# Two transformer blocks on one core: the second block's attention, gate and first query in another order

## The reference, cut to what matters

```python
x = rms(x, final_norm)                               # end of the first block
h = rms(x, ln_mix_g)
u, v, q, k, vb = split(h @ w_in_2)                   # 5 x 512 columns
# gate: per block of 128 tokens and group g of 64 columns
v  = rms(gelu(v), gmlp_norm_g)
sp = einsum('gij,bnjgc->bnigc', masked w_s, v) + b_s
a  = gelu(u) * sp
# band attention: 8 heads of 64, chunks of 64 see themselves and 8 before
q, k = rms per head (q, q_g), rms per head (k, k_g)
p  = softmax(q k^T / 8 + rel_bias, masked)
x  = x + concat(a, p @ vb) @ w_out_2
# experts: 8 heads choose 16 of 16384 experts for each token
qq = rms(x, ln_ffn_g) @ w_query                      # 2048 columns
sc = qq . sub_keys;  16 best of 128, twice;  16 best of the 256 sums -> eidx, g = softmax
x  = x + sum_k g_k * gelu(u[eidx_k] . rms(x)) * v[eidx_k]
```

## Time and profile before

| | |
|---|---|
| median of 3 runs | 1234.54 us |
| the profiled execution's own time | 1229.8 us |
| its span, first to last instruction | 1228.1 us |
| TensorE busy | 1066.6 us (87%) |
| VectorE busy | 809.1 us (66%) |
| ScalarE busy | 614.0 us (50%) |
| GpSimd busy | 344.3 us (28%) |
| mean granted TensorE clock | 0.975 of full speed |
| DMA moved | 369.54 MB, 301 GB/s |

### The profile page before, as it was taken

One profiled execution on the slowest core, in us unless ns is written; L12 is line 12 of the kernel. 1 busy time (PEld: TensorE's weight loads), 2 busy tenths in 40 slices (PEclk: granted clock), 3 DMA queues, 4 the chain that ended last, 5 costly groups with the idle time before them and its releaser, 6 DMA issues.

```text
span 1228.1 us, 12558 instructions
## 1 busy us (share of the span) xinstructions
PE 1066.6 (87%) x3760; PEld 664.6 (54%) x3760; DVE 809.1 (66%) x1669; ACT 614.0 (50%) x1340; POOL 344.3 (28%) x288
## 2 busy tenths in 40 slices
PE   6999999999999999999878988777778777778686
PEld 5788878788878777877434443323223323233232
DVE  4763666665545677567786677766776677677744
ACT  6464554454445456656555544544344434544453
POOL 1000000200000000016556444444545454555440
PEclk9999999999999999899999999999999998989999
DMA  8453447765625653336999999999999999999995
GB/s 309 138 198 111 138 144 237 262 201 176 188 87 193 220 203 101 140 137 232 422 421 422 421 421 421 422 421 419 422 422 415 422 415 408 409 413 423 422 420 244
DMA packets 95253, 369.54 MB, mean 301 GB/s; under 512 B 6544, under 2 KB 30104, under 8 KB 62304
## 3 DMA queue, kind: packets, MB, share of 16 engines
q0 software_dynamic: 38176, 273.46, 54.0%
q1 hardware_dynamic: 57024, 95.44, 23.3%
HBM read 367.81 MB, written 1.06 MB: 300 GB/s over the span
## 4 chain that ended last, share of the span: by engine, by line
PE 48%; DMA 24%; DVE 15%; ACT 6%; issue 3%; POOL 1%; DVEq 0%; SPq 0%; ACTq 0%
DMA uv_ring<-in_peer_uv,expert 24%; PE gemm L1633 12%; PE gemm L1312 10%; PE gemm L1314 10%; PE gemm L1313 10%; DVE uv_ring L1228 4%; PE trb L1306 1%; DVE w_lo L769 1%; ACT w_hi L440 1%; POOL uv_ring L418 1%; ACT diag L739 1%; PE mmb L1392 1%; DVE hit L1218 1%; PE mmb L1433 1%; DVE hit L1216 1%
## 5 line engine op out<-in xcount | busy, mean ns | idle before, releaser
L1633 PE MATMUL gemm<-uv_ring,diag 128*128 128x512 f32 x1024 | 499.0, 632 | 126.6 <-ACT diag L739 126.4
L1633 PEld LDWEIGHTS gemm<-uv_ring,diag 128*128 128x128 f32 x1024 | 192.1, 199 | 421.1 <-ACT diag L739 246.2
L1228 DVE CUSTOM_DVE_ANT_0 uv_ring<-uv_ring,xn 128x1024 f32<-128x1024 f32 x256 | 310.1, 1222 | 160.3 <-DMA uv_ring<-in_peer_uv,expert 159.8
L418 POOL DMA_INDIRECT uv_ring<-in_peer_uv,expert x256 | 317.5, 1240 | 324.2 <-PE gemm L1633 302.6
L769 DVE TENSOR_TENSOR w_lo<-raw,w_hi 128x1024 fp32r<-128x1024 f32 (+1 forms) x197 | 208.6, 1072 | 167.8 <-ACT w_hi L440 167.1
L440 ACT ACTIVATE w_hi<-raw 128x1024 fp32r<-128x1024 f32 (+1 forms) x204 | 189.1, 939 | 198.0 <-PE gemm L1314 195.7
L1312 PE MATMUL gemm<-w_hi,hT_hi 128*128 128x512 f32 (+1 forms) x608 | 247.0, 406 | 16.7 <-DVE w_lo L769 15.6
L1314 PE MATMUL gemm<-w_hi,hT_lo 128*128 128x512 f32 (+1 forms) x608 | 237.5, 391 | 0.0
L1313 PE MATMUL gemm<-w_lo,hT_hi 128*128 128x512 f32 (+1 forms) x608 | 236.9, 390 | 0.0
L733 ACT ACTIVATE hid_g<-hid,scales 128x1 f32<-128x1 f32 x256 | 75.1, 293 | 312.0 <-DVE hid L1228 309.9
L1312 PEld LDWEIGHTS gemm<-w_hi,hT_hi 128*128 128x128 f32 x608 | 115.5, 190 | 44.0 <-DVE w_lo L769 17.0
(11 more groups left out here) (203 smaller groups left out, 776.9 us busy)
## 6 DMA issues: line engine op xcount, KB each, us to landing
raw<-in_w_in SPq DMA_DIRECT2D x31, 1024.0 KB, 5.2
raw<-in_w_gate SPq DMA_DIRECT2D x22, 512.0 KB, 3.9
raw<-in_w_up SPq DMA_DIRECT2D x22, 512.0 KB, 4.9
raw<-in_w_down SPq DMA_DIRECT2D x22, 512.0 KB, 3.2
raw<-in_w_out SPq DMA_DIRECT2D x8, 1024.0 KB, 5.0
raw<-in_peer_w_query SPq DMA_DIRECT2D x8, 1024.0 KB, 5.0
raw<-in_w_ret_o SPq DMA_DIRECT2D x4, 1024.0 KB, 5.1
uv_ring<-in_peer_uv,expert POOLq DMA_INDIRECT x256, 14.4
```

Source lines behind the costliest of these rows:

```text
L418: nc.gpsimd.indirect_dma_start(out=uv_ring[k % RING][:], out_offset=None, in_=peer_uv, in_offset=bass.IndirectOffsetOnAxis(ap=expert[:, n, ...
L1228: V.tensor_tensor_reduce(out=u_row, in0=u_row, in1=xn[:, b, :], scale=1.0, scalar=0.0, op0=ALU.mult, op1=ALU.add, accum_out=hid[par][:, k: ...
L1633: last = nc.tensor.matmul(gemm[2 * b + n][:], diag[k % 4][:], uv_ring[k % RING][:, D + n * CHUNK:D + (n + 1) * CHUNK], start=(begin and k ...
```

## The change

It reorders, with these parts:

- norm2 and norm4: the remainders of quarters 2 and 3 of C_FF and C_QUERY are VectorE's and stand before the gain of tile 1; at norm2 tile 0's inverse root stands after tile 1's columns, and TensorE turns tile 1 before quarter 3 instead of quarter 2.
- norm3 and C_IN2 + 1: quarters of roundings and remainders stand between the columns, the squares and the roots.
- Band: the turns of q and k and the score jobs stand between the parts of C_IN2 + 3 and C_IN2 + 4. The turned k is ScalarE's, as before.
- The probabilities are turned undivided; the division is in the eviction of the attention result, now VectorE's. They are turned before the gate product.
- Gate: 8 matmuls of 128 columns (both tiles), evicted by 8 fused operations (add the bias, multiply by u) into `proj2`; `sq` isn't used and `mixed_a_ready` goes. TensorE order: gate, values of tile 0, turns, values of tile 1, C_OUT2.
- ScalarE makes tile 1's exponentials after the gelu of v and its squares.
- GpSimd loads the keys once the band's q and k are normed.
- C_QUERY: tile 0's four quarters first, then tile 1's turns, tile 0's query turned, its key scores, then tile 1.

```diff
-            remainders(C_FF, (2, 3))
-            pool.wait_ge(mixed_a_ready, TB)
+            pool.wait_ge(qk_normed, TB)
             pool.dma_start(keys_t[:], peer_keys_t).then_inc(keys_landed, 16)
-            remainders(C_QUERY, (2, 3))
             remainders(C_QUERY + 1, (1, 2, 3))
...
# ScalarE, norm_behind
+                hi_at(c + 1, quarters=(2, 3))
                 squares(0, 1)
-                hi_at(c + 1, quarters=(2, 3))
-                root_of(name, 0)
-                residual_in(c, 1)
-                hi_columns(name, (2, 3))
-                squares(1, 1)
-                root_of(name, 1)
+                if name == "norm4":
+                    root_of(name, 0)
+                else:
+                    residual_in(c, 1)
+                    hi_columns(name, (2, 3))
+                    root_of(name, 0)
+                    squares(1, 1)
+                    root_of(name, 1)
...
# ScalarE, second block
+            hi_at(C_IN2, quarters=(0, 1))
             hi_columns("norm3", (0, 1))
-            hi_at(C_IN2)
+            hi_at(C_IN2, quarters=(2, 3))
...
+            hi_at(C_IN2 + 3)
+            in2_out(2)
+            key_columns(0)
             hi_at(C_IN2 + 4, quarters=(0,))
+            key_columns(1)
+            hi_at(C_IN2 + 4, quarters=(1,))
             softmax_exp(2, 0)
-            hi_at(C_IN2 + 4, quarters=(1,))
-            softmax_exp(2, 1)
             hi_at(C_IN2 + 4, quarters=(2, 3))
+            in2_out(3, ACT.Gelu_apprx_tanh)
...
+            softmax_exp(2, 1)
             root("gate", TB)
             nc.scalar.preload_act_table(ACT.Gelu_apprx_tanh)
+            probs_columns((0, 1))
+            in2_out(4, ACT.Gelu_apprx_tanh)
+            probs_columns((2, 3, 4, 5))
             hi_at(C_OUT2)
...
             queries_out(0, 0)
+            residual_in(C_OUT2 + 1, 1)
+            hi_columns("norm4", (2, 3))
             query_columns(0, 0)
-            hi_at(C_QUERY + 1, quarters=(0,))
+            squares(1, 1)
+            root_of("norm4", 1)
             scores_out(0, 0)
-            hi_at(C_QUERY + 1, quarters=(1, 2, 3))
+            hi_at(C_QUERY + 1)
...
# VectorE, norm_behind
+                lo_at(c + 1, quarters=(2, 3))
+                if name == "norm4":
+                    variance(name, 0)
+                    inverse_root(0, 1, RS[name], dst=scales[:, at:at + 1], done=scale_ready)
                 gained(1, 0, row)
-                variance(name, 0)
-                inverse_root(0, 1, RS[name], dst=scales[:, at:at + 1], done=scale_ready)
                 residual(c, 1, (1,), scale)
                 gained(1, 1, row)
                 lo_columns(name, (2, 3))
+                if name == "norm2":
+                    variance(name, 0)
+                    inverse_root(0, 1, RS[name], dst=scales[:, at:at + 1], done=scale_ready)
...
# VectorE, second block
             down_in(0)
+            lo_at(C_IN2, quarters=(0,))
             lo_columns("norm3", (0, 1))
-            lo_at(C_IN2, quarters=(0, 1))
+            lo_at(C_IN2, quarters=(1,))
             down_in(1)
...
+            lo_at(C_IN2 + 3, quarters=(0,))
+            query_band(0)
+            lo_at(C_IN2 + 3, quarters=(1,))
+            query_band(1)
+            lo_at(C_IN2 + 3, quarters=(2, 3))
+            band_scores((0, 1))
+            band_max(0, 2)
+            lo_at(C_IN2 + 4, quarters=(0,))
+            band_scores((2, 3))
+            lo_at(C_IN2 + 4, quarters=(1,))
+            band_scores((4, 5))
+            band_max(1, 6)
+            lo_at(C_IN2 + 4, quarters=(2, 3))
...
-            finish_softmax()
...
+            def band_out(b):
+                m = MM["o_band"] + b
                 dve.wait_ge(mm_filled, m + 1)
+                V.tensor_tensor(proj2[:, b, D:D + HALF]..., mmb[m % 2][:]..., den[:, b, :].unsqueeze(2).to_broadcast([P, HEADS, HD]), ALU.mult)
+            for n in range(2):
+                m = MM["gate"] + n
+                for g in range(4):
+                    u = proj2[:, :, (4 * n + g) * HD:(4 * n + g + 1) * HD]
+                    V.scalar_tensor_tensor(out=u, in0=mmb[m % 2][:, g * P:(g + 1) * P]..., scalar=gains[:, G_BS + ...], in1=u, op0=ALU.add, op1=ALU.mult)
+            lo_at(C_OUT2, quarters=(0, 1))
+            band_out(0)
+            lo_columns("mixed", (0, 1))
+            lo_at(C_OUT2, quarters=(2, 3))
+            band_out(1)
+            lo_columns("mixed", (2, 3))
...
# TensorE
-            product_at(C_FF, by_tile=True, ready=columns_ready("norm2"), before={(2, 0): norm_columns("norm2", 1)})
+            product_at(C_FF, by_tile=True, ready=columns_ready("norm2"), before={(3, 0): norm_columns("norm2", 1)})
...
+            product_at(C_IN2 + 3, before={(0, 0): lambda: turn_band(0, 0), (0, 1): lambda: turn_band(0, 1), (1, 0): lambda: turn_band(1, 0),
+                                          (1, 1): lambda: turn_band(1, 1), (2, 0): lambda: score_band((0, 1)), (3, 0): lambda: score_band((2, 3))})
+            product_at(C_IN2 + 4, before={(0, 0): lambda: score_band((4, 5))})
+            for n in range(6): ... turn(TR["p_band"] + n, ...)
+            for n in range(2):
+                bank = mm_bank(MM["gate"] + n)
+                for g in range(4):
+                    at = HALF + (4 * n + g) * HD
+                    nc.tensor.matmul(bank[:, g * P:(g + 1) * P], ws_t[:, 4 * n + g, :], proj2[:, :, at:at + HD], start=True, stop=True)
+            band_values(0)
+            columns("mixed", mixed_rows, (0, 1))
+            band_values(1)
+            product_at(C_OUT2, before={(1, 0): lambda: columns("mixed", mixed_rows, (2, 3))}, ready=columns_ready("mixed"))
...
             product_at(C_QUERY, by_tile=True, ready=columns_ready("norm4"),
-                       before={(2, 0): norm_columns("norm4", 1), (1, 1): lambda: turn_queries(0, (0,)), (2, 1): lambda: key_scores(0, (0,))})
+                       before={(0, 1): lambda: (norm_columns("norm4", 1)(), turn_queries(0, (0,)), key_scores(0, (0,)))})
```

133 lines of the change are left out of this document (64 added, 69 removed).

## The result

The changed kernel takes 1212.24 us by the median of 4 executions (1211.61 to 1212.95), the kernel before 1233.91 on the same chip (1228.26 to 1236.47); the ratio is 0.9839, 95% interval [0.9815, 0.9864]. The forecast was 1222.5 with a range of 1217.5 to 1229: the direction was right, the gain about twice what I had said. The changed kernel's profiled execution took 1212.02 us (span 1210.2, granted clock 0.98) against 1229.8, so the traces explain 17.8 of the 21.7 us between the medians.

The account below looks back on a forecast made before the run. TensorE was taken to bound the work ahead of the first gather, DMA the 660 us after it. Five gains sum to 14.1 us, less 2 set aside; 12 off the median 1234.54 gives 1222.5, range 1217.5 to 1229.

Parts of the forecast that it names:

- The median of the runs shown is 4.7 above that execution; less 12: Whole kernel: 12 us taken off the median 1234.54, which lay 4.7 above the profiled execution, gives 1222.5.
- Against it I set 2: Allowance against the summed gains: 1.7 us for a clock fall on the gate's chain, 0.3 for releases rounded off.
- Rival A: Whole kernel: everything in the sum and no clock fall, 14 to 15 us off, 1220; chance 0.15.
- The sum of the parts: Ahead of the first gather: five gains of 3.9, 2.0, 2.6, 5.2 and 0.4 us, 14.1 together.
- Part 4: Last band product to C_OUT2's first matmul: division at eviction, earlier turns and a shorter gate save 5.2 us.
- Part 2: Second block's input (norm3): an earlier start and no wait at the next product save 2.0 us.
- part 5: norm4 and first query product: tile 0's query first saves 0.4 us, select then held by a remainder.
- Part 3: Band: turns and scores between product parts save 2.6 us, the block taking 32.5 us.
- Rival C: Band products: DVE becomes the bound, each insertion waits 1 us, 7 us back, 1229.5; chance 0.09.
- B: Clock falls for the whole gate chain and at tile 0's query, 3.5 us more lost, 1226; chance 0.11.
- D: Expert phase: gathers run slower, at 408 GB/s throughout, 20 us more, 1242.9; chance 0.04.
- E: Expert phase: the start moves but not the end, 2 us off or less, 1233; chance 0.04.

Follow-up runs that it names:

- b2_before: The kernel before, unaltered, profiled once more: 1234.02 us.
- x1_tables: Changed kernel with two more ScalarE table loads between the band's last exponential and the gate's root: 1215.56 us.
- u7_bandexp: Changed kernel with band turns and scores in one piece and tile 1's exponentials ahead of the next product's roundings and gelus, as before: 1220.96 us.
- u1_norm2: Changed kernel with norm2's orders as before and GpSimd's first two remainders back: 1216.36 us.
- u4_divide: Changed kernel with the probabilities divided before they are turned and the attention result evicted by a plain copy: 1218.92 us.
- u6_gate64: Changed kernel with the gate tile by tile as before, 16 matmuls of 64 columns instead of 8 of 128: 1215.13 us.
- u2_norm3: Changed kernel with norm3 as before, columns first, then roundings and remainders in one piece: 1217.83 us.
- c3_bandfilled: Changed kernel with band turns and scores in one piece and eight spare matmuls in that piece's gaps: 1220.40 us.
- c1_filled: Kernel before with 29 spare matmuls in TensorE's waits at norm2, norm3, the gate and norm4: 1229.25 us.

## Why the prediction was wrong

The median forecast was 10.3 us too high. In the terms of its sum:

- **"The median of the runs shown is 4.7 above that execution; less 12": 4.5 us, and the step that failed.** I took the distance between median and profiled execution as a constant of the kernel and carried it over to the new one. It isn't: after, the distance is 0.2, and of the kernel before's 4.7 some 2 came from its three timed executions, as the median over 74 is 1232.6, 2.8 above mine. What the traces show of that distance is time at half clock, which profiled executions of one kernel have in different amounts (10.2 us in mine, 23.9 in b2_before) and the changed kernel's have not at all; that the timed ones differ by the same is inferred.
- **"Against it I set 2": 2.0 us.** I looked at what the change makes idle (494 to 499) and set a fall against the sum. No fall came ahead of the gathers in the changed kernel's two traces. The waits that are left in the gate's chain are 0.34, 0.97 and 0.52 us; with 2.1 us more at the first of them (x1_tables) the clock does fall there, for 6.8 us. Rival A, with 0.15, had this part right.
- **The start: 2.2 us.** The profiled execution of before reached the first edit later than any of the other traces. One trace can't show that.
- **The sum of the parts: 15.4 for 14.1.** Part 4 gave 0.8 more: I put ScalarE's table load behind the maximum, but it runs ahead of the wait for it. In the changed kernel tile 1's load starts at 479.41, the maximum comes at 480.40 and the first exponential follows at 480.70, so 1.0 of the load's 1.28 us is hidden; for tile 0 the load was 2.53 us early:

```profile
465.78 1.28 ACT L478 ACT_TABLE_LOAD   x1
469.59 0.40 ACT L478 ACTIVATE probs<-probs,neg_mx 128x128 f32<-128x128 f32 x1 [2.53 <-DVE neg_mx L1166]
...
479.41 1.28 ACT L478 ACT_TABLE_LOAD   x1
480.70 0.51 ACT L478 ACTIVATE probs<-probs,neg_mx 128x256 f32<-128x256 f32 x1
```
```profile
480.23 0.17 DVE L1166 TENSOR_SCALAR neg_mx<-mx 128x8 f32<-128x8 f32 x1
```

But the step's size is luck in part: I priced the new order at full clock against 19.1 us and a gate of 5.9 that had the fall of 6.8 us in them, and never named it as a term there. Against 16.2, the same work without the fall, the order gives 3.1 us of the 6.0. The gate's 1.95 us and the waits on ScalarE were as forecast; the fused ops take 0.343 us each, within my 0.2 to 0.5. Part 2 gave 0.6 more, since only 1.12 us of wait stayed at its first product; part 5 gave 0.6 more with its own order right, select's first copy directly behind the remainder that waited for ScalarE, as forecast. Part 3 gave 0.9 less in these two traces: the wait of 0.97 us on the remainder came as said, the block is 33.20 and not 32.5. Those four numbers are the table's, not tested singly but for the undoings above.

These are 4.5 + 2.0 + 2.2 + 1.3, with 0.3 of the expert phase: 10.3. Undone one at a time, the parts cost 4.0, 2.5, 7.9 (u7_bandexp), 6.67 and 2.6 (the two halves of part 4) and 1.0 in the stretch, 24.7 together, where all of them are worth 15.4. The falls in these traces (u1_norm2 3.4 us, u7_bandexp 10.2, u4_divide 10.2, u6_gate64 3.4) are about 12 of it by the prices above, an estimate; without them it is some 12 to 13, against 11 for the change without falls. So a single gap that comes back can bring a fall, and each undoing pays for its own.

Rival C (VectorE's insertions wait 1 us each) was wrong, there was one such wait. B, D and E were wrong too: no fall in the gate's chain, the gathers at 413 GB/s in 1000 to 1100 where they had 408, and the end of the kernel moved with the start. A had the absence of a fall right and, built on the same 4.7, the time wrong (1220). What stays open: that the clock falls in the timed executions of u2_norm3, and how often it does in those of the kernel before, is inferred from medians, the groups of u7_bandexp and five profiled executions, since a timed execution leaves no stages; and why one gap is followed by a fall in one execution and not in the next, no run here shows. The changed order isn't proof against falls either: three of its variants (c3_bandfilled, u4_divide, u6_gate64) have one at norm4.

## What to carry to other kernels

When the median lies well above the profiled execution and executions scatter, profile the unchanged kernel again a few times before pricing a change: compare time at half clock part by part, take the part's length without a fall as its base, and measure from a mark ahead of the first edit. A wait of TensorE ahead of a product can cost more than its length, since a fall of the clock may follow it, so spreading small matmuls between parts of products can pay beyond its arithmetic. A single gap filled or opened doesn't price the fall, since another gap may have one in that run. When an undoing costs far more than expected, look first at which other engine's order came back only halfway.

## What the runs showed of the hardware

- Half clock for 10.2 us in the band's block costs 4.7 us there (39.72 against 35.04) and for 13.7 us 6.2 (41.1 against 34.9); 6.8 us around the gate cost 2.4 to 3.0, 3.4 us at norm2, norm3 or norm4 1.3 to 1.6. TensorE is the bound in these places, so somewhat under half of the time at half clock is lost.
- TensorE fed with matmuls whose result is thrown away kept the clock where waiting lost it (c3_bandfilled at 464, c1_filled at 238), without time of its own that a median could show; one trace each.
- A table load on ScalarE ran before the wait of the activation that needs it (load at 465.78, the exponential behind the maximum at 469.59), so it is free where that wait is longer than 1.28 us.
